# Latent attention on one Trainium2 core: value products issued for two steps at a time

## The chip, the cores and the metric

The kernel runs on 1 core of one Trainium2 chip. The metric is device time in microseconds (us). The engines are TensorE (PE in the rows, its weight loads PEld), VectorE (DVE), ScalarE (ACT), GpSimd (POOL) and SyncE (SP). The time before is 3274.03 us, the median of three runs (3273.06 to 3274.99).

## The reference, cut to what matters

The program is a two-layer block with three branches (convolution, mLSTM, latent attention) over 512 tokens and 256 context tokens, followed by a second block. Only the attention is touched: 8 heads, queries and keys of 64 plain and 32 rotated features, values of 64 features.

```python
def mla_attend(qn, qr, kn, kr, v):
    s = jnp.einsum('bqhd,bkhd->bhqk', qn, kn) + jnp.einsum('bqhr,bkr->bhqk', qr, kr)
    p = jax.nn.softmax(s.astype(jnp.float32) * MLA_SCALE, axis=-1).astype(v.dtype)
    return jnp.einsum('bhqk,bkhd->bqhd', p, v)
...
    o_x = mla_blockwise(qn_x, qr_x, jnp.concatenate([kn_c, kn_x], 1), jnp.concatenate([kr_cc, kr_x], 1),
                        jnp.concatenate([vv_c, vv_x], 1))
...
    o_c = mla_attend(qn_c, qr_c, kn_c, kr_cc, vv_c).reshape(bsz, uc.shape[1], MLA_HEADS * V_HEAD)
```

The last line (attention of the context tokens over themselves) is computed in the first layer only.

## The kernel before

`attention_stage(core, l)` is run for layer 0 (`both` is true: tokens and context are queries) and for layer 1 (tokens alone). The eight heads go in four pairs p = 0 to 3; j = 0 and 1 is the head in the pair. Keys go in six tiles of 128, and each key tile is one **step** i of its pair: i = 0 to 5. In layer 0 a seventh step, i = 6, holds the context queries (`items` is 7 there, 6 in layer 1). g counts the steps through all pairs: 28 in layer 0, 24 in layer 1.

What one step does, each part named by its function:

- `score(g, j)`: the scores of head j, transposed (128 keys x 512 queries) in one PSUM bank per head. Pair 0 uses plain fp32 (L1676); the other pairs split queries and keys in a high and a low part and add three fp32r products (L1679, L1680, L1681). It waits for the exponential of the same head one step before (`exp_ready`, at 2g - 1 + j), which frees the bank.
- `exponent(g, j)` on ACT (L1795): exponential of the bank into one of four `probs` tiles, tile (2g + j) % 4. From g = 2 on it first waits until the value products of step g - 2 are done (`attended`, at g - 1) and until the sums of step g - 2 are added.
- `add(g, j)` on POOL (L1914, L1917; L1910 for the context): the running sum of the exponentials, from which the softmax's denominator comes.
- `attend(g)`: the value products, probabilities times values. Both heads write one bank, head 0 in partitions 0 to 63 and head 1 in 64 to 127 (L1732; L1739 for the context step, i = 6). Each of the two products shows in the trace as two matmuls, so a step shows as four.
- `unit(p + 1, u)`: the rough scores of the next pair, from which the row maxima come (L1618, for the context L1622), one or two per step (`units_of`). Unit u waits for the maximum of unit u - 2. `maximum` on DVE (L1964) reads each one. The last of them lets `turn_rows` (L1631) put the maxima on the queries' rows; ACT and DVE copy the rows (L1815, L1969), and the next pair's first scores wait for these copies.
- `total(p, ctx)`: the sums of the exponentials over the partitions (L1718). In layer 1 it stands in step 1 of the next pair, and after the last step.
- In layer 0 steps 2 and 4 hold modulation products as well (`mod_rows_pair`, L787, and `turn_mods`, L796); a `turn_mods` of a pair before the last waits for the third or fifth maximum of its pair.

DVE also computes the low parts of the next pair (`query_low` L1973, `key_low` L1978), reciprocals of the sums (L2000) and copies of results and totals (L1985, L1994), in the fixed order in which they are written. ACT rounds the next pair's queries and keys (L1800, L1805) in steps 0 and 1; unit 0 waits for that.

The order on PE is written out by hand in one loop over g: `score(g, 0)`, first unit, `score(g, 1)`, `attend(g - 1)`, second unit, and what the step has besides. So the value products run one step behind the scores:

```python
            score(g, 1)
            if g:
                attend(g - 1)
            if second is not None:
                unit(p + 1, second)
```

Of the kernel before, what the change touches and what calls it, by code (L numbers as in the profile page):

```python
# [1439 lines left out]
def attention_stage(core, l):  # L1440

    nc, both = core.nc, l == 0
# [53 lines left out]
    def at_group(kind, n):  # L1497

        g = HEAD_GROUPS[l].index((kind, n))
        return g // 4, g % 4  # L1500
# [9 lines left out]
    steps_of = [(p, i) for p in range(PAIRS) for i in range(items)]  # L1510
# [5 lines left out]
    def unit_at(p, i, j):  # L1516

        return units_of.get(i, (None, None))[j] if p + 1 < PAIRS else None
# [9 lines left out]
    mod_steps = [g for g, (p, i) in enumerate(steps_of) if both and i in (2, 4)]  # L1528
    n_steps = len(mod_steps)
    assert 2 * n_steps == n_mods  # L1530
    halves = [(0, TC), (TC, TX)]
    lows_at = {1: [("query", 0)], 3: [("key", 0)], 4: [("query", 1)], 5: [("key", 1)]} if both else \
        {2: [("query", 0), ("key", 0)], 4: [("query", 1), ("key", 1)]}
# [14 lines left out]
    def _(pe):  # L1548
# [10 lines left out]
        def turn_mods(b):  # L1559
            pe.wait_ge(mod_copied.sem, mod_copied.at(b + 1))  # L1560
            return turn_mod_rows(core, pe, lambda pair: mod_rows, 1, mod_sums[:, 4 * b:4 * b + 4])
# [121 lines left out]
        def score(g, j):  # L1683
            p, i = steps_of[g]
            if g:
                pe.wait_ge(s["exp_ready"].sem, s["exp_ready"].at(2 * g - 1 + j))
            elif j == 0:

                pe.wait_ge(s["v_copied"].sem, s["v_copied"].at(1))
                pe.wait_ge(s["v_copied_by_act"].sem, s["v_copied_by_act"].at(1))  # L1690
            copied = s["odd_rows_copied" if j else "rows_copied"]
            if i == 0:
                pe.wait_ge(copied.sem, copied.at(row_sets * p + 1))
                if j == 0:
                    pe.wait_ge(s["kr_copied"].sem, s["kr_copied"].at(2 * p + 2))
                if in_parts[p]:
                    for low in (s["query_low"], s["key_low"]):
                        pe.wait_ge(low.sem, low.at(2 * p - 2 + j + 1))
            if i < NT:
                mm = scored_tile(scores[j], p, j, slice(i * P, (i + 1) * P), slice(0, TX))  # L1700
            else:
                pe.wait_ge(copied.sem, copied.at(row_sets * p + 2))
                for x in range(NT - NTX):
                    mm = scored_tile(scores[j][:, x * TC:(x + 1) * TC], p, j, slice(TX + x * P, TX + (x + 1) * P), slice(TX, T))
            mm.then_inc(s["scored"].sem, 1)

        def total(p, ctx):

            n = p * closings + ctx
            pe.wait_ge(s["added"].sem, s["added"].at(adds_until(p, NT if ctx else NT - 1, 1)))  # L1710
            last_ctx = ctx and p + 1 == PAIRS
            if both and not ctx:
                pe.wait_ge(mod_copied.sem, mod_copied.at(2 * p + 2))
            if n and not last_ctx:
                pe.wait_ge(s["totals_copied"].sem, s["totals_copied"].at(n))
            for j in range(2):
                source, to = (ctx_sums[j], last_totals if last_ctx else totals[:, 0:TC]) if ctx else (sums[j], totals)
                mm = pe.matmul(to[j * VH:(j + 1) * VH, :], core.ones[:, 0:VH], source, start=True, stop=True, skip_group_check=True)  # L1718
            mm.then_inc(s["totaled"].sem, 1)

        def attend(g):
            p, i = steps_of[g]
            n = p * closings
            pe.wait_ge(s["exp_ready"].sem, s["exp_ready"].at(2 * g + 2))
            if g == 0:
                pe.wait_ge(s["v_copied"].sem, s["v_copied"].at(3))
                pe.wait_ge(s["v_copied_by_act"].sem, s["v_copied_by_act"].at(3))
            if i < NT:
                if i == 0 and p:
                    pe.wait_ge(s["result_copied"].sem, s["result_copied"].at(n))  # L1730
                for j in range(2):
                    mm = pe.matmul(result[j * VH:(j + 1) * VH, :], values[:, i, 2 * p + j, :], probs[(2 * g + j) % 4],  # L1732
                                   start=(i == 0), stop=(i == NT - 1), skip_group_check=True)
            else:
                if p + 1 < PAIRS:
                    pe.wait_ge(s["result_copied"].sem, s["result_copied"].at(n + 1))
                for x in range(NT - NTX):
                    for j in range(2):
                        mm = pe.matmul(ctx_results[p][j * VH:(j + 1) * VH, :], values[:, NTX + x, 2 * p + j, :],  # L1739
                                       probs[(2 * g + j) % 4][:, x * TC:(x + 1) * TC], start=(x == 0), stop=(x == NT - NTX - 1),  # L1740
                                       skip_group_check=True)
            mm.then_inc(s["attended"].sem, 1)

        for g, (p, i) in enumerate(steps_of):
            first, second = unit_at(p, i, 0), unit_at(p, i, 1)
            score(g, 0)
            if p and i == 1 and not both:
                total(p - 1, 0)
            if i == items - 1 and p + 1 < PAIRS:
                turn_rows(p + 1, 0)  # L1750
            if first is not None:
                if g == 1:
                    pe.wait_ge(s["v_copied_by_act"].sem, s["v_copied_by_act"].at(3))
                unit(p + 1, first)
            score(g, 1)
            if g:
                attend(g - 1)
            if second is not None:
                unit(p + 1, second)
            if both and i == NT:  # L1760
                total(p, 0)
            elif both and i == 0 and p:
                total(p - 1, 1)
            if g in mod_steps:
                b = mod_steps.index(g)
                if b:
                    if p + 1 < PAIRS:
                        pe.wait_ge(s["max_ready"].sem, s["max_ready"].at((p + 1) * len(units) + (3 if i == 2 else 5)))
                    turn_mods(b - 1)
                else:  # L1770
                    pe.wait_ge(s["v_copied"].sem, s["v_copied"].at(3))
                if p:
                    pe.wait_ge(s["totals_copied"].sem, s["totals_copied"].at(closings * p))
                mod_rows_pair(core, pe, run, *at_group("mod", 2 * b), mod_in)
            if i == 0 and both:
                turn_rows(p, 1)
        attend(len(steps_of) - 1)
        total(PAIRS - 1, closings - 1)
        if both:
            turn_mods(n_steps - 1).then_inc(mod_turned.sem, 1)  # L1780
# [3114 lines left out]
```

## Time and profile before

| what | before |
|---|---|
| median of three runs | 3274.03 us (3273.06 to 3274.99) |
| the profiled execution's own time | 3270.61 us |
| its span | 3268.8 us |
| PE busy | 3169.7 us, 97% of the span |
| DVE / POOL / ACT busy | 2012.1 / 1199.2 / 1182.1 us |
| steps of the attention in layer 0 | 397 to 508 us of the span |
| steps of the attention in layer 1 | 1819 to 1907 us of the span |

The span is that of one execution under the profiler. A row of the timeline gives the start in us from the span's start, how long the merged instructions took together, the engine, the line of the kernel, what they write and read, their number, and in brackets how long the engine had been idle and what released it. Starts of matmuls are the better guide: the end of one is modelled, and it overlaps the next.

### The profile page before, as it was taken

How to read it: one execution, taken by the hardware profiler on the slowest of the kernel's cores; microseconds unless marked ns; L12 is line 12 of the kernel's file. 1: busy time of each engine (PE TensorE's matmuls, PEld its weight loads, DVE VectorE, ACT ScalarE, POOL GpSimd, SP SyncE). 2: the span in 40 equal slices, each digit the busy share in tenths (PEclk: the TensorE clock that was granted, in tenths of full speed). 3: DMA queues.
4: the chain of work that ended last, by engine and by line, in shares of the span. 5: the costliest groups of instructions: out<-in, count | busy, mean ns of one | idle time of the engine just before them, and what ended most of it. 6: DMA issues, size and time to landing. Idle time of an engine off the chain costs nothing. (4 is left out here: it accounts for less than half of the span.)

```text
span 3268.8 us, 46548 instructions
## 1 busy us (share of the span) xinstructions
PE 3169.7 (97%) x17058; PEld 2552.7 (78%) x17058; DVE 2012.1 (62%) x2954; ACT 1182.1 (36%) x1672; POOL 1199.2 (37%) x607
## 2 busy tenths in 40 slices
PE   8999999999999999999999989999999998999998
PEld 7888557888888888887776467778998766788886
DVE  6957565448877424257996653678533675777634
ACT  3232444522243223133543444234322364322223
POOL 3332155233333222232431453543444314344442
PEclk9999999999999999999999999999999999999999
DMA  6222120234412222222222003652333221333332
GB/s 227 58 58 52 48 78 20 55 103 152 147 57 66 60 63 65 62 62 72 76 78 55 7 1 110 195 172 85 97 91 97 78 77 52 91 96 90 94 98 79
DMA packets 467677, 271.75 MB, mean 83 GB/s; under 512 B 53937, under 2 KB 453297, under 8 KB 466354
## 3 DMA queue, kind: packets, MB, share of 16 engines
q1 hardware_dynamic: 467362, 269.36, 28.0%
q8 instruction: 119, 1.95, 0.3%
q14 instruction: 52, 0.43, 0.0%
q10 hardware_dynamic: 144, 0.02, 0.0%
HBM read 267.21 MB, written 2.10 MB: 82 GB/s over the span
## 5 line engine op out<-in xcount | busy, mean ns | idle before, releaser
L390 POOL TENSOR_TENSOR weights_low<-weight_ring,weights_high 128x1024 fp32r<-128x1024 f32 (+1 forms) x403 | 979.4, 2431 | 1719.7 <-ACT weights_high L381 1718.6
L381 ACT ACTIVATE weights_high<-weight_ring 128x1024 fp32r<-128x1024 f32 (+1 forms) x408 | 410.2, 1006 | 1071.2 <-PE ps L491 1006.8
L486 PE MATMUL ps<-features_high,weights_high 128*128 128x512 f32 (+1 forms) x1888 | 638.9, 353 | 8.3 <-DVE features_low L2759 4.6
L487 PE MATMUL ps<-features_low,weights_high 128*128 128x512 f32 (+1 forms) x1888 | 635.2, 353 | 0.0
L486 PEld LDWEIGHTS ps<-features_high,weights_high 128*128 128x128 f32 x1888 | 355.0, 188 | 68.1 <-DVE features_low L2759 5.7
L487 PEld LDWEIGHTS ps<-features_low,weights_high 128*128 128x128 f32 x1888 | 354.7, 188 | 55.0 <-issue 0.2
L491 PE MATMUL ps<-features_high,weights_low 128*128 128x512 f32 (+1 forms) x1888 | 384.3, 351 | 0.0
L486 PE MATMUL ps<-u_high,weights_high 128*128 128x512 f32 (+2 forms) x944 | 369.5, 395 | 8.8 <-DVE z L3814 2.6
L487 PE MATMUL ps<-u_low,weights_high 128*128 128x512 f32 (+2 forms) x944 | 363.0, 389 | 0.0
L491 PEld LDWEIGHTS ps<-features_high,weights_low 128*128 128x128 f32 x1888 | 305.3, 188 | 47.3
L1337 DVE SCALAR_TENSOR_TENSOR conv<-conv,vectors 128x512 f32<-128x512 f32 (+1 forms) x480 | 307.2, 707 | 5.5 <-DVE conv L1337 3.9
L486 PE MATMUL ps<-mlp_u_high,weights_high 128*128 128x512 f32 (+1 forms) x960 | 269.2, 310 | 0.9 <-DVE arena L3604 0.9
L487 PE MATMUL ps<-mlp_u_low,weights_high 128*128 128x512 f32 (+1 forms) x960 | 267.1, 310 | 0.0
L3546 DVE SCALAR_TENSOR_TENSOR x_features<-ps,modulation,x_features 128x512 f32<-128x512 f32 x118 | 74.9, 661 | 266.1 <-PE ps L491 254.6
L491 PE MATMUL ps<-u_high,weights_low 128*128 128x512 f32 (+2 forms) x944 | 227.8, 384 | 0.0
L486 PEld LDWEIGHTS ps<-u_high,weights_high 128*128 128x128 f32 (+1 forms) x944 | 180.1, 191 | 56.1 <-issue 10.9
L487 PEld LDWEIGHTS ps<-u_low,weights_high 128*128 128x128 f32 (+1 forms) x944 | 180.1, 191 | 39.5 <-issue 1.4
L491 PEld LDWEIGHTS ps<-u_high,weights_low 128*128 128x128 f32 (+1 forms) x944 | 171.0, 188 | 38.3 <-issue 0.5
L486 PEld LDWEIGHTS ps<-mlp_u_high,weights_high 128*128 128x128 f32 x960 | 180.9, 188 | 13.7 <-ACT weights_high L381 1.0
L487 PEld LDWEIGHTS ps<-mlp_u_low,weights_high 128*128 128x128 f32 x960 | 180.7, 188 | 10.8
L3482 ACT ACTIVATE arena<-arena,seam 128x512 f32<-128x512 f32 x96 | 59.1, 647 | 287.4 <-DVE arena L3628 287.4
L491 PE MATMUL ps<-mlp_u_high,weights_low 128*128 128x512 f32 (+1 forms) x960 | 150.9, 309 | 0.0
(638 smaller groups left out, 4960.9 us busy)
## 6 DMA issues: line engine op xcount, KB each, us to landing
weight_ring<-in_w SPq DMA_DIRECT2D x256, 256.0 KB, 3.0
weight_ring<-in_w_in SPq DMA_DIRECT2D x246, 256.0 KB, 3.3
conv<-in_w_mod_columns SPq DMA_DIRECT2D x64, 512.0 KB, 4.7
weight_ring<-in_w_up SPq DMA_DIRECT2D x88, 256.0 KB, 3.1
weight_ring<-in_w_out SPq DMA_DIRECT2D x48, 256.0 KB, 3.1
weight_ring<-in_w_mod SPq DMA_DIRECT2D x32, 256.0 KB, 3.5
weight_ring<-in_w_down SPq DMA_DIRECT2D x32, 256.0 KB, 3.0
first_modulation<-in_first_modulation SPq DMA_DIRECT2D x4, 1024.0 KB, 9.5
```

The lines of the kernel that those rows point to most:

```text
L381: act.activation(core.ring_high[:, split_slot(run, q), 0:n], core.ring[:, slot, 0:n], ACT.Copy).then_inc(core.high_ready.sem, 1)
L390: pool.tensor_tensor(core.ring_low[:, split_slot(run, q), 0:n], core.ring[:, (run.first + q) % SLOTS, 0:n], high.bitcast(F32), ALU.subtrac ...
L486: pe.matmul(to, w_high[:, k, 0:m], high(k, a, b), start=(first and k == ks[0]), stop=False, skip_group_check=True)
L487: pe.matmul(to, w_high[:, k, 0:m], low(k, a, b), start=False, stop=False, skip_group_check=True)
L491: mm = pe.matmul(out[:, at:at + b - a], w_low[:, k, 0:m], high(k, a, b), start=False, stop=(last and k == ks[-1]), skip_group_check=True)
L1337: nc.vector.scalar_tensor_tensor(conv[:, f, a:b], pads[:, f, bass.ds(t + at, b - a)], w_dw[:, bass.ds(t, 1), f], conv[:, f, a:b], ALU.mult ...
L3482: ins = act.activation(tmp[:, a:b], pre_of[own(i, q)][:, a:b], ACT.Relu, bias=cols_of[own(i, q)][:, ns + j:ns + j + 1])
L3546: ins = nc.vector.scalar_tensor_tensor(x, gemm(core, q % 2)[:, a:b], mod[:, gates + q, j:j + 1], x, ALU.mult, ALU.add)
```

## The change

The value products are no longer issued in every step. A table of the step's number i says which steps' products stand behind `score(g, 1)`: at i = 2 and i = 4 (and i = 6 in layer 0) those of the two steps before, one behind the other; at i = 0 in layer 1 those of the last two steps of the pair before, in layer 0 the context step's alone. At i = 1, 3 and 5 there are none. In layer 1 the last two steps' products stand together behind the loop, as they did before. Nothing else is moved, and waits and buffers are as they were.

```diff
+    values_behind = lambda g: [] if g == 0 else {0: [g - 1] if both else [g - 2, g - 1], 2: [g - 2, g - 1], 4: [g - 2, g - 1],
+                                                 6: [g - 2, g - 1]}.get(steps_of[g][1], [])
...
             score(g, 1)
-            if g:
-                attend(g - 1)
+            for of in values_behind(g):
+                attend(of)
             if second is not None:
...
-        attend(len(steps_of) - 1)
+        for of in [len(steps_of) - 1] if both else range(len(steps_of) - 2, len(steps_of)):
+            attend(of)
         total(PAIRS - 1, closings - 1)
```

In the changed kernel the lines behind the table are two higher (L1734 is the old L1732, L1681 to L1683 are L1679 to L1681, L1620 is L1618). The names: L1679 to L1681 are one head's scores, L1618 a unit, L1732 the value products, L1718 the totals, L1631 `turn_rows`.

PE in layer 1, third pair (p = 2), from the second head's scores of step 3 to those of step 5, before:

```order
L1679 MATMUL ps<-query_part_13156,features_high 128x512
L1680 MATMUL ps<-features_low,features_high 128x512
L1681 MATMUL ps<-query_part_13156,features_high 128x512
L1732 MATMUL ps<-ranks 64x512 x2
L1618 MATMUL ps<-weights_high,weights_low 128x512
L1618 MATMUL ps<-weights_high,weights_low 128x256
L1679 MATMUL ps<-features_low,features_high 128x512
L1680 MATMUL ps<-features_low,features_high 128x512
L1681 MATMUL ps<-features_low,features_high 128x512
L1618 MATMUL ps<-weights_high,weights_low 128x512
L1618 MATMUL ps<-weights_high,weights_low 128x256
```

The same place in the changed kernel, one step further, to the second head's scores of step 4, the value products and the second unit behind them:

```order
L1681 MATMUL ps<-query_part_13156,features_high 128x512
L1682 MATMUL ps<-features_low,features_high 128x512
L1683 MATMUL ps<-query_part_13156,features_high 128x512
L1734 MATMUL ps<-ranks 64x512 x4
L1620 MATMUL ps<-weights_high,weights_low 128x512
L1620 MATMUL ps<-weights_high,weights_low 128x256
```

In step 3 the products are gone; in step 4 four stand between the second scores and the last unit, where two stood.

PE in layer 1 at the passage from the third pair to the last, from `turn_rows` of step 5 to the value products of the next step 0, before:

```order
L1631 MATMUL ps<-constants,conv 33x128 x4
L1679 MATMUL ps<-query_part_13156,features_high 128x512
L1680 MATMUL ps<-features_low,features_high 128x512
L1681 MATMUL ps<-query_part_13156,features_high 128x512
L1732 MATMUL ps<-ranks 64x512 x2
L1679 MATMUL ps<-weights_low,weights_high 128x512
L1680 MATMUL ps<-features_low,weights_high 128x512
L1681 MATMUL ps<-weights_low,features_high 128x512
L1679 MATMUL ps<-weights_low,weights_high 128x512
L1680 MATMUL ps<-features_low,weights_high 128x512
L1681 MATMUL ps<-weights_low,features_high 128x512
L1732 MATMUL ps<-ranks 64x512 x2
```

and in the changed kernel:

```order
L1633 MATMUL ps<-constants,conv 33x128 x4
L1681 MATMUL ps<-query_part_13156,features_high 128x512
L1682 MATMUL ps<-features_low,features_high 128x512
L1683 MATMUL ps<-query_part_13156,features_high 128x512
L1681 MATMUL ps<-weights_low,weights_high 128x512
L1682 MATMUL ps<-features_low,weights_high 128x512
L1683 MATMUL ps<-weights_low,features_high 128x512
L1681 MATMUL ps<-weights_low,weights_high 128x512
L1682 MATMUL ps<-features_low,weights_high 128x512
L1683 MATMUL ps<-weights_low,features_high 128x512
L1734 MATMUL ps<-ranks 64x512 x4
```

The products of step 4 moved from behind the scores of step 5 to behind those of the next pair's step 0, beside the products of step 5.

## Rows read from the trace of the kernel before

**Rows 1.** The page, busy time and instructions of each engine.
```profile
PE 3169.7 (97%) x17058; PEld 2552.7 (78%) x17058; DVE 2012.1 (62%) x2954; ACT 1182.1 (36%) x1672; POOL 1199.2 (37%) x607
```

**Rows 2.** Windows, one pair of each kind: third of layer 0, second and last of layer 1.
```profile
core 0: us, PE busy (x) PEld busy (x) DVE busy (x) ACT busy (x) POOL busy (x), PEclk, DMA share, GB/s
455.00:484.00 29.00, 27.75 (x190) 16.52 (x188) 21.28 (x24) 13.43 (x22) 18.31 (x14) 1.00 0.26 74
1842.00:1864.00 22.00, 20.94 (x89) 10.51 (x88) 17.17 (x17) 10.24 (x17) 14.84 (x12) 1.00 0.00 1
1886.00:1907.00 21.00, 19.07 (x74) 8.04 (x72) 5.67 (x7) 7.16 (x12) 15.05 (x12) 1.00 0.00 1
```

**Rows 3.** Timeline of PE, layer 1: scores, value products alone, then together, totals.
```profile
1889.16 0.40 PE L1680 MATMUL ps<-features_low,weights_high 96*128 96x512 f32 x1
...
1893.90 0.40 PE L1681 MATMUL ps<-weights_low,features_high 96*128 96x512 f32 x1
1894.23 1.08 PE L1732 MATMUL ps<-ranks 128*64 128x512 f32 x4
1895.24 0.50 PE L1679 MATMUL ps<-weights_low,weights_high 97*128 97x512 f32 x1
1895.58 0.40 PE L1680 MATMUL ps<-features_low,weights_high 96*128 96x512 f32 x1
1895.81 0.39 PE L1681 MATMUL ps<-weights_low,features_high 96*128 96x512 f32 x1
...
1902.05 1.94 PE L1732 MATMUL ps<-ranks 128*64 128x512 f32 x8
1905.76 1.08 PE L1718 MATMUL ps<-ranks,ones 128*64 128x512 f32 x4 [1.78 <-POOL ranks L1917]
```

**Rows 4.** Timeline of DVE, layer 1, third pair.
```profile
1869.09 0.96 DVE L1964 TENSOR_REDUCE conv<-ps 128x1 f32<-128x768 f32 x1 [1.75 <-PE ps L1618]
1869.97 0.68 DVE L1994 COPY conv<-ps 128x512 f32<-128x512 f32 x1
1871.34 0.96 DVE L1964 TENSOR_REDUCE conv<-ps 128x1 f32<-128x768 f32 x1 [0.69 <-PE ps L1618]
1872.21 1.74 DVE L2000 RECIPROCAL conv<-conv 128x256 f32<-128x256 f32 x1
1873.87 1.75 DVE L1964 TENSOR_REDUCE conv<-ps 128x1 f32<-128x768 f32 x2
...
1881.49 1.75 DVE L1964 TENSOR_REDUCE conv<-ps 128x1 f32<-128x768 f32 x2
```

**Rows 5.** Timeline of PE, layer 1, third pair: products, second unit; later `turn_rows`.
```profile
1872.97 1.08 PE L1732 MATMUL ps<-ranks 128*64 128x512 f32 x4
1873.98 0.62 PE L1618 MATMUL ps<-weights_high,weights_low 96*128 96x512 f32 x2
...
1883.29 1.06 PE L1631 MATMUL ps<-constants,conv 128*33 128x128 f32 x8 [0.64 <-DVE conv L1964]
```

**Rows 6.** Timelines of ACT and of POOL, layer 1, last pair.
```profile
1893.64 1.30 ACT L1795 ACTIVATE ranks<-ps 128x512 f32<-128x512 f32 x2 [1.31 <-PE ps L1681]
1896.24 1.30 ACT L1795 ACTIVATE ranks<-ps 128x512 f32<-128x512 f32 x2 [1.31 <-PE ps L1681]
...
1894.31 7.73 POOL L1917 TENSOR_TENSOR ranks<-ranks 128x512 f32<-128x512 f32 x6 [0.63 <-ACT ranks L1795]
1902.00 1.27 POOL L1923 TENSOR_TENSOR features<-features,conv 128x512 f32<-128x512 f32 x1
1903.23 2.48 POOL L1917 TENSOR_TENSOR ranks<-ranks 128x512 f32<-128x512 f32 x2
```

**Rows 7.** Timelines, layer 0: PE in the first pair; DVE, then PE in the third.
```profile
421.62 1.06 PE L1631 MATMUL ps<-constants,conv 128*33 128x128 f32 x8 [0.19 <-DVE conv L1964]
...
459.36 1.75 DVE L2000 RECIPROCAL conv<-conv 128x256 f32<-128x256 f32 x1
461.14 0.96 DVE L1964 TENSOR_REDUCE conv<-ps 128x1 f32<-128x768 f32 x1
...
478.10 0.28 PE L1681 MATMUL ps<-features_low,features_high 96*128 96x256 f32 x1
479.62 1.06 PE L1631 MATMUL ps<-constants,conv 128*33 128x128 f32 x8 [1.25 <-DVE conv L1964]
...
481.77 1.08 PE L1732 MATMUL ps<-ranks 128*64 128x512 f32 x4
```

**Rows 8.** A wait of PE, and windows around it and behind the first attention.
```profile
1714.04 1.18 PE L1104 MATMUL ps<-constants,arena 36*128 36x36 f32 x16 [1.92 <-ACT gates L1216]
...
1716.20:1722.90 6.70, 6.70 (x28) 5.90 (x28) 6.08 (x12) 0.00 (x0) 1.17 (x1) 0.50 0.01 2
477.00:481.00 4.00, 2.75 (x21) 2.27 (x20) 3.74 (x5) 0.87 (x2) 4.00 (x4) 1.00 0.52 152
```

## The prediction

> **What bounds the kernel now.** I read the busy times first [rows 1]: PE is busy for 97% of the span, so time is saved where PE gets shorter and lost where PE waits. The change lies in two stretches, 397 to 508 us and 1819 to 1907 us, about 6% of the span. The windows [rows 2] show PE busy for 27.75 of 29, 20.94 of 22 and 19.07 of 21 us there. That is an average, so I went on to the timelines, to see which wait ends last at each place. Two other engines are close. In layer 1's third pair DVE starts its second maximum at 1871.34 and from then on runs one operation behind the other until the last maximum, which ends at 1883.24 [rows 4]; 0.05 us later `turn_rows` starts, at 1883.29, after PE waited [rows 5]. So from the second unit to `turn_rows` DVE sets the time. In layer 1's last pair POOL adds, divides and adds without a gap from 1894.31 to 1905.71, and the total on PE starts at 1905.76 after waiting 1.78 us for it [rows 3, 6]. That tail is POOL's.
>
> **What one merge saves.** [rows 3] have both cases. Score products follow each other at 0.23 us (1895.58 to 1895.81). A value block alone begins 0.33 us after the last score product (1893.90 to 1894.23), the next product starts 1.01 us after the block (1895.24), and the one after that 0.34 us later (1895.58) in place of 0.23. So a block alone puts 0.33 + 1.01 - 0.23 + 0.11 = 1.22 us between scores. Behind the last step two blocks already touch: eight matmuls take 1.94 us, four take 1.08, so the second costs 0.86. A merge saves 1.22 - 0.86 = 0.36, say 0.35 us. In layer 0, 24 blocks become 12; in layer 1, 23 become 12, since the last two touch already. 12 + 11 merges by 0.35 are 8.0 us: the most that the change can give, 0.25% of the run.
>
 Taken as the whole story, the rule makes this the first rival below.
>
> **Layer 0, pair 0** (397 to 426 us). PE sets the pace (even `turn_rows` waits only 0.19 us for DVE [rows 7]), so its three merges pay 1.05 us. But `turn_rows` in step 6 waits for DVE, and what stood ahead of it and could be hidden is moved behind it: going through the steps with 1.22 and 0.86 I get the first unit pairs earlier, the last maximum 1.5 us earlier, and the next pair's first scores 0.7 us earlier. **-0.7 us.**
>
> **Layer 0, pairs 1 and 2.** Here `turn_rows` waits 1.25 us for the last maximum (478.10 plus 0.28 against 479.62) [rows 7]. In step 5 the value products of step 4 stand in that wait's shadow and cost nothing. After the change they stand behind `turn_rows`, beside those of step 5, and cost 0.86. Ahead of it DVE is limited by its own order: the merge of step 2 buys nothing, because unit 2, which now comes sooner, waits for the first maximum, and that one stands behind a reciprocal of 1.75 us [rows 7]; the merge of step 4 brings DVE forward by some 0.25 us. 0.86 - 0.25 = 0.6 us each, two pairs: **+1.2 us.**
>
> **Layer 0, pair 3** has no units and no `turn_rows`. Three merges would give 1.05 us. But a new wait appears: `exponent(g, 0)` needs the value products of step g - 2, which in an even step now stand behind `score(g, 1)`. The next scores of that head need this exponential. From the start of two blocks, the first is done after about 1.07 us and the exponential after another 0.65; the scores come 1.87 us after the start. That fits with 0.1 us to spare. In the odd steps scores come two after two with no products between. A head's scores start at 1895.24 and their exponential at 1896.24 [rows 3, 6]: 1.0 us, and 0.65 for the exponential, make a round trip of 1.65, while PE has 0.8 + 0.7 = 1.5 us of scores to fill it. That is 0.15 us of waiting, two or three times in the pair. I leave -0.45 us. **Layer 0 together: -0.7 + 1.2 - 0.45 = 0.05 us.**
>
> **Layer 1, pairs 0 and 1.** In pair 0 the merges are eaten by unit 6, which waits for the maximum of unit 4 once units come sooner; the next pair begins 0.26 us early. Through pair 1 the same DVE chain holds, with unit 1 over 1 us earlier (no products ahead of it) and the last unit as late as before behind two blocks. At the end of it the lead is about 0.15 us. The double block (steps 4 and 5) then stands in step 0 of pair 2, ahead of unit 0.
>
> **Layer 1, pair 2.** Unit 0 comes 0.86 - 0.15 = 0.7 us later, and its maximum starts at 1869.8 in place of 1869.09. The totals' copy stands behind it [rows 4], so the second maximum starts at 1871.3, as before, although its unit is there earlier. In step 2 the second unit stands behind two blocks: it starts at 1874.3 in place of 1873.98 [rows 5], and the fourth maximum 0.3 us later, since DVE had started that one almost at once. Unit 6 waits for the fifth maximum and inherits the 0.3; the double block of step 4 follows, and unit 7 ends only about 1883.1, where DVE would have begun its maximum at about 1882.3 [rows 4]. So `turn_rows` starts about 0.85 us late, at 1884.15, and behind it the double block costs another 0.86: the first scores of step 1 of the last pair are 1.7 us late.
>
> **Layer 1, pair 3.** Step 1 has no products now, so PE makes good 1.0 us: the scores of step 2 are only 0.65 us late (1893.3). But their exponential no longer follows them. It waits for the first of the two value blocks behind the second head's scores: those scores at 1894.1, the block at 1894.9, done 1.07 us later, so the exponential starts at 1896.0 in place of 1893.64, and POOL's first add at 1896.65 in place of 1894.31 [rows 6], 2.35 us late. From there POOL has the same six adds, one division and two adds, 11.4 us without a gap. The total starts 2.35 us late, and the stage ends with it. **Layer 1: +2.35 us.** No later merge can win it back, since POOL, not PE, ends this stage.
>
> **The sum.** 0.05 + 2.35 = 2.4 us. The profiled execution took 3270.61 us itself, which would become 3273.0; it lies 3.4 us under the median of the runs, 3274.03, and against that the forecast is **3276.4 us**. A measurement of this kernel can tell about 0.2%, 6.5 us, from no change, so the likeliest outcome is none that can be told. No instruction, transfer or queue entry is added; SP's order and its waits for free weight slots are the same, and the modulation weights' slots come free within 0.5 us of before. Bounds of the unknown part: the round trip of an exponential could cost nothing (then pairs 3 of both layers keep their merges: layer 0 0.6 us better, layer 1 still tied to POOL), or 0.3 us more at each of the 24 double blocks, 7 us worse. The DVE stretches could give 1 us back or take 1 us more.
>
> **Rivals.**
>
> *A. PE keeps every merge* (chance 0.12). The drains go away and neither DVE nor POOL is in the way: 3274.03 - 8.0 = 3266.0 us. For it: PE is busy 97%, and no row shows DVE at work for a whole pair (17.17 of 22 us [rows 2]). Against it: `turn_rows` waits for DVE in the later pairs of both layers, and the total waits for POOL [rows 3, 5, 7].
>
> *B. The longer waits bring TensorE's clock down* (chance 0.13). In layer 0, pairs 1 and 2, PE reaches step 6 earlier while `turn_rows` stays with DVE: its wait of 1.25 us grows to about 2.4. Today the granted clock stays at 1.00 over that wait; but a single wait of 1.92 us at 1714.04 is followed by 6.7 us at 0.50, 1.2 GHz in place of 2.4 [rows 8]. PE work in such a stretch takes twice as long, so each costs up to 3.4 us. Twice: 3276.4 + 6.8 = 3283.2 us, 0.28% slower than before. It decides if the wait reaches about 1.9 us and the clock's check falls on it. Against it: PE is dense on both sides of the wait.
>
> The Trainium skill (TensorE: Matmul & The Clock Gate, What's actually happening) says that TensorE's clock is set by how busy it was recently. [rows 8] agree for the wait at 1714; whether this wait is enough no row shows.
>
> *C. The POOL tail does not grow* (chance 0.2): the start of the last pair is less late than I think, or POOL finds gaps to close. Then the gains and losses cancel: 3274 us.
>
> That the change does not do what it says is excluded: the order on PE shows the four products together in the even steps.
>
> **How the numbers follow.** My forecast has 0.55 (3272 to 3279.5 us by itself), A 0.12, B 0.13, C 0.2. Faster by over 0.2% is A, 0.12; slower by over 0.2% is B, 0.13; the rest, 0.75, lies within 0.2%. The range reaches from 3268.5, which leaves out the full gain of A, to 3283.5, which takes in B.
>
> **What would show it.** Right: a value block of eight matmuls in 1.94 us everywhere; `turn_rows` in layer 1's third pair 0.8 us later after the pair's start than now; the first add of POOL's closing run 2.3 us later than now and the run still 11.4 us without a gap; PE's wait before `turn_rows` in layer 0's third pair about 2.4 us; first scores of the last pair in layer 0 some 0.5 us later. Wrong: a stage in layer 1 that ends earlier than 1906.8, a granted clock under 1.00 inside either stretch, or exponentials that hold up the scores in every even step.

## The result, and the profile after

The changed kernel took 3296.13 us (median of 4 runs, 3293.77 to 3296.55), the kernel before beside it 3273.66 us (4 runs, 3273.06 to 3274.99): **a ratio of 1.0066, 95% interval 1.0051 to 1.0081, 22.5 us slower.** That lies beyond the range of the prediction. The profiled execution took 3293.77 us with a span of 3291.9.

The two traces run level (within 0.15 us) up to the first attention. Behind layer 0's attention PE is 6.2 us late, at the first product behind layer 1's 21.9 us; at the end of the span it is 23.1. So nearly the whole loss lies in the two stretches that the change touches. I measure a stage from its first `turn_rows` to the first product of what follows: layer 0 goes from 120.6 to 127.0 us, layer 1 from 95.6 to 111.3 us.

The page of the changed kernel answers to [rows 1]: as many instructions as before, but PE is busy for 9.3 us longer, since part of the same work now runs at a lower clock.

```profile
PE 3179.0 (97%) x17058; PEld 2560.7 (78%) x17058; DVE 2019.4 (61%) x2954; ACT 1179.3 (36%) x1672; POOL 1201.2 (36%) x607
```

Windows over the two attention stages before, columns as in [rows 2]:

```profile
399.00:513.90 114.90, 106.12 (x706) 59.07 (x706) 69.86 (x80) 48.74 (x82) 66.92 (x55) 0.99 0.26 73
1815.70:1911.30 95.60, 85.07 (x329) 39.05 (x329) 56.82 (x56) 40.14 (x67) 58.22 (x44) 0.98 0.02 6
```

and the same of the changed kernel, then three windows inside them:

```profile
398.80:520.10 121.30, 109.45 (x706) 63.24 (x706) 71.31 (x80) 47.44 (x82) 64.62 (x55) 0.93 0.24 69
1821.90:1933.20 111.30, 90.62 (x329) 42.31 (x329) 63.03 (x56) 38.71 (x66) 60.38 (x44) 0.91 0.02 5
...
455.00:484.00 29.00, 26.21 (x182) 16.40 (x179) 19.93 (x22) 13.11 (x22) 17.35 (x14) 0.97 0.26 74
449.00:455.80 6.80, 6.31 (x22) 3.83 (x24) 2.70 (x4) 0.38 (x1) 0.51 (x1) 0.50 0.01 2
1892.80:1899.60 6.80, 6.00 (x14) 2.33 (x15) 4.08 (x4) 1.09 (x2) 2.03 (x2) 0.50 0.00 0
```

Two things stand out. The mean granted clock (the column PEclk) falls from 0.99 to 0.93 and from 0.98 to 0.91: there are six new stretches at 0.50, which is 1.2 GHz in place of 2.4, two in layer 0 (449.0 and 483.1, 6.8 us each) and four in layer 1 (1841.6, 1869.0 and 1906.5, 3.4 us each, and 1892.8, 6.8 us). And DVE is busy for 6.2 us more in layer 1, with no more work to do.

PE's timeline of the changed kernel shows a longer wait just ahead of each of those stretches, or around its start. First `turn_rows` of layer 0's third pair, which answers to [rows 7], and the products behind it; then unit 6 of layer 1's third pair, with score products and a value block behind it; then the last total, which answers to [rows 3]:

```profile
479.44 0.28 PE L1683 MATMUL ps<-features_low,features_high 96*128 96x256 f32 x1
482.19 1.06 PE L1633 MATMUL ps<-constants,conv 128*33 128x128 f32 x8 [2.47 <-DVE conv L1967]
483.18 0.80 PE L1624 MATMUL ps<-weights_high,weights_low 96*128 96x256 f32 x2
...
1890.70 0.39 PE L1683 MATMUL ps<-features_low,features_high 96*128 96x512 f32 x1
1893.60 1.01 PE L1620 MATMUL ps<-weights_high,weights_low 96*128 96x512 f32 x2 [2.51 <-DVE conv L1967]
1894.40 0.63 PE L1681 MATMUL ps<-query_part,features_high 97*128 97x512 f32 x1
1894.83 0.63 PE L1682 MATMUL ps<-features_low,features_high 96*128 96x512 f32 x1
1895.82 3.68 PE L1734 MATMUL ps<-ranks 128*64 128x512 f32 x8
...
1927.68 1.08 PE L1720 MATMUL ps<-ranks,ones 128*64 128x512 f32 x4 [2.67 <-POOL ranks L1920]
```

A block of eight value products takes 3.68 us behind that wait, and 1.94 us where the clock is at 1.00. The other three stretches of layer 1 stand at waits of 1.98 us (unit 6 of the first pair, 1841.39), 2.48 us (unit 6 of the second, 1867.89) and 1.71 us. The last of these is at a place that the prediction didn't look at: behind `turn_rows` the second head's first scores wait for DVE's copy of the row of maxima (L1972, the old L1969):

```profile
1905.62 0.47 PE L1681 MATMUL ps<-weights_low,weights_high 97*128 97x512 f32 x1 [1.71 <-DVE weights_low L1972]
```

DVE's timeline, layer 1, third pair, shows what unit 6 waited for:

```profile
1888.32 0.96 DVE L1967 TENSOR_REDUCE conv<-ps 128x1 f32<-128x768 f32 x1 [0.32 <-PE ps L1620]
1889.19 1.54 DVE L1976 TENSOR_TENSOR features_low<-features,weights_low 96x512 fp32r<-96x512 f32 x1
1890.66 2.02 DVE L1981 TENSOR_TENSOR features_high<-features,weights_high 96x768 fp32r<-96x768 f32 x1
1892.60 1.81 DVE L1967 TENSOR_REDUCE conv<-ps 128x1 f32<-128x768 f32 x2
```

The two tensor-tensor operations form the low parts of queries and keys (`query_low`, `key_low`). In the first pair of the kernel before, DVE does the same shapes in 0.68 and 0.95 us:

```profile
1838.41 0.68 DVE L1973 TENSOR_TENSOR features_low<-features,weights_low 96x512 fp32r<-96x512 f32 x1
1839.01 0.95 DVE L1978 TENSOR_TENSOR features_high<-features,weights_high 96x768 fp32r<-96x768 f32 x1
```

POOL's timeline of the changed kernel has at that time four adds in one run, over both operations; and in the last pair the closing run, which answers to [rows 6]:

```profile
1887.65 6.15 POOL L1920 TENSOR_TENSOR ranks<-ranks 128x512 f32<-128x512 f32 x4 [1.86 <-ACT ranks L1798]
...
1916.33 7.63 POOL L1920 TENSOR_TENSOR ranks<-ranks 128x512 f32<-128x512 f32 x6 [1.43 <-ACT ranks L1798]
1923.92 1.26 POOL L1926 TENSOR_TENSOR features<-features,conv 128x512 f32<-128x512 f32 x1
1925.15 2.48 POOL L1920 TENSOR_TENSOR ranks<-ranks 128x512 f32<-128x512 f32 x2
```

In the kernel before, POOL's adds of the second pair (and of the third, 22.3 us later) come as two and, 0.8 us behind them, three; query's low part (1853.25 to 1853.93) lies in the gap between them but for its last 0.2 us, and key's runs into the three:

```profile
1850.42 2.52 POOL L1917 TENSOR_TENSOR ranks<-ranks 128x512 f32<-128x512 f32 x2 [0.98 <-ACT ranks L1795]
1853.74 4.60 POOL L1917 TENSOR_TENSOR ranks<-ranks 128x512 f32<-128x512 f32 x3 [0.80 <-ACT ranks L1795]
```

ACT's timeline of the changed kernel has the source of the run of four. Two exponentials, which wait for the merged value products, follow each other at once, and two more come behind them; before they stood 1.05 us apart or more:

```profile
1886.97 1.09 ACT L1798 ACTIVATE ranks<-ps 128x512 f32<-128x512 f32 x2 [1.31 <-issue]
1889.03 0.60 ACT L1798 ACTIVATE ranks<-ps 128x512 f32<-128x512 f32 x1 [0.97 <-PE ps L1683]
1890.08 0.60 ACT L1798 ACTIVATE ranks<-ps 128x512 f32<-128x512 f32 x1 [0.46 <-PE ps L1683]
```

### The profile page after: what moved, and what is told of

Its sections match the earlier page's. It is cut to its first block and busy times, and to the rows that moved or that the text cites. A ratio compares the mean times of both kernels' runs of the same rounds, so it can differ in the third digit from the quotient of the medians.

```text
span 3291.9 us, 46548 instructions
## 1 busy us (share of the span) xinstructions
PE 3179.0 (97%) x17058; PEld 2560.7 (78%) x17058; DVE 2019.4 (61%) x2954; ACT 1179.3 (36%) x1672; POOL 1201.2 (36%) x607
```

## The experiments

Three causes are weighed: that the granted clock falls behind longer waits; that DVE and POOL hinder each other, since the adds are bunched; and that only the order on PE costs, as in the prediction.

### One layer at a time

```diff
+    merged = values_behind
+    values_behind = merged if both else (lambda g: [g - 1] if g else [])    (layer0_only)
+    values_behind = (lambda g: [g - 1] if g else []) if both else merged    (layer1_only)
-        for of in [len(steps_of) - 1] if both else range(len(steps_of) - 2, len(steps_of)):
+        for of in [len(steps_of) - 1]:                                      (layer0_only)
```

> The merged order in layer 0 alone, layer 1 as before. The changed kernel's trace is 6.2 us behind the old one from the end of layer 0's attention on, with two new stretches of 6.8 us at a granted clock of 0.50 in pairs 1 and 2. Theory (the two attentions are independent): 3273.7 + 6 = about 3280 us, with those two stretches again. Rival (the whole 22 us comes from how later clock stretches fall after a shift): 3290 us or more, or none of it.

> The merged order in layer 1 alone, layer 0 as before. Theory: 3273.7 + 16 = about 3290 us; waits of PE of about 2.5 us before the seventh unit of pairs 1 and 2, and stretches of low clock behind them. Rival (phase only): since layer 0 does not shift the later part by 6 us, the low stretches fall elsewhere and the cost is under 8 us.

Measured: layer 0 alone 3279.79 us (3277.35 to 3282.10, 10 runs) against 3275.67 (17 runs), ratio 1.0012 [1.0003, 1.0022]; layer 1 alone 3289.22 us (3284.24 to 3293.49, 6 runs), 1.0037 [1.0024, 1.0049]. So 4.1 and 13.6 us: each layer's part makes the kernel slower, the second by more, and the untouched layer keeps its length (95.66 and 120.63 us). The two do not add up to 22.5 us. The traced execution of layer 1 alone was the slowest of its six; its stage took 114.6 us, with five low stretches where the changed kernel has four in 111.3. In the profile of layer 0 alone the clock fell in one pair only, 124.1 us for the stage in place of 127.0. That gives a comparison of two like pairs in one execution, the second and the third, same order, with and without the low clock:

```profile
429.70:462.60 32.90, 30.10 (x190) 18.17 (x188) 20.60 (x24) 13.09 (x23) 17.37 (x14) 0.90 0.22 64
462.60:492.40 29.80, 27.02 (x190) 16.86 (x188) 20.65 (x24) 12.42 (x22) 17.38 (x14) 1.00 0.25 72
```

One fall costs 3.1 us. It came in one of two like places. The runs of these kernels also scatter by 5 and 9 us, which would fit with falls that come in one execution and not in another; only one execution of each has a trace, so that is not shown.

### The changed order, with the waits filled

Head 0's score products are issued again just ahead of the longer waits; they write the same values once more, so PE is at work where it had been idle. The first attempt also repeated second heads' scores in layer 0, behind the wait; the second one doesn't.

```diff
+            again = (1 if j else 4 if p in (1, 2) and i == NT else 1) if both else
+                {(0, 4): 3, (1, 4): 4, (2, 4): 4, (1, 0): 2, (2, 0): 2, (3, 0): 2}.get((p, i), 1) if j == 0 else 1
-                mm = scored_tile(scores[j], p, j, slice(i * P, (i + 1) * P), slice(0, TX))
+                for _ in range(again):
+                    mm = scored_tile(scores[j], p, j, slice(i * P, (i + 1) * P), slice(0, TX))
```

> The changed order in both layers, but where PE would wait it repeats the products of the first head's scores (which its exponential does not follow at once in those steps), 2 to 4 times over, so that PE has work in the waits. Theory clock (the longer waits bring the clock down and the work behind them runs at 1.2 GHz): the new low stretches, 30.6 us in all, vanish, and with them 10 to 15 us: 3281 to 3286 us. What is left over 3274 is the order's own cost on DVE and POOL. Rival order (DVE and POOL chains set the whole loss and the clock falls only where nobody waits for PE): 3294 us or more, as the repeats only add work.

> The changed order with PE kept busy in its waits, this time with the first head's scores alone repeated (in the first such kernel layer 0's second heads were repeated too, behind the wait, at 2.1 us in each of two pairs). Theory clock plus order: no stretch of low clock inside either attention; layer 0's stage 0.5 us longer than before (121.1 us against 120.63 from the first row turn to the next stage), layer 1's 8 us longer (104 against 95.6). About 3282 us. Rival (the order costs nothing once the clock stays up): 3274 to 3276 us.

Measured: the first 3286.41 us (3282.89 to 3288.34, 6 runs) against 3275.67, 1.0028 [1.0016, 1.0041]; the second 3284.01 us (3280.61 to 3284.68, 6 runs) against 3274.31 (12 runs), 1.0032 [1.0019, 1.0044]. Neither has a low stretch in an attention before its end. Windows of the second one over both stages, and over layer 1's second and third pair:

```profile
399.00:514.20 115.20, 107.72 (x741) 64.62 (x740) 71.38 (x79) 47.26 (x81) 64.64 (x54) 0.99 0.26 73
1816.30:1920.30 104.00, 90.88 (x361) 46.24 (x360) 63.36 (x57) 38.76 (x67) 60.49 (x44) 0.98 0.02 6
1840.70:1865.50 24.80, 23.44 (x100) 13.31 (x101) 19.21 (x18) 10.02 (x18) 14.60 (x11) 1.00 0.00 1
1865.50:1890.20 24.70, 23.17 (x101) 13.32 (x101) 19.16 (x18) 9.78 (x18) 16.09 (x12) 1.00 0.00 1
```

With 67 more products recorded on PE the kernel loses 9.7 us to the one before in place of 22.5. So the clock's part is shown, in both layers. By stage, filling takes 6.0 us from layer 0 (126.96 to 120.97) and 7.3 from layer 1 (111.34 to 104.01): 13.3 us, beside 12.8 in the medians. What is left is 0.34 us in layer 0 and 8.4 in layer 1, and the clock can't explain those: it stands at 1.00 up to the last value products. Nor do the repeated products add to PE's path in layer 1: PE still waits for DVE behind them, 0.27 to 0.43 us before unit 6 and 0.6 to 0.75 us before the second heads' first scores.

### POOL's adds made short, in either order

From the third step of a pair on, the adds cover 32 of 512 columns, and the add of the second step only copies one operand, scaled by 1. What is left out are the sums of the exponentials over the steps.

```diff
-                ins = nc.gpsimd.tensor_tensor(sums[j], probs[(2 * g - 2 + j) % 4], here, ALU.add)
+                ins = nc.gpsimd.tensor_scalar(sums[j], here, 1.0, None, ALU.add)
...
-                ins = nc.gpsimd.tensor_tensor(sums[j], sums[j], here, ALU.add)
+                ins = nc.gpsimd.tensor_tensor(sums[j][:, 0:32], sums[j][:, 0:32], here[:, 0:32], ALU.add)
```

> The old order; GpSimd's running sums are left out but for 32 of 512 columns (from a pair's third step on), so that GpSimd is nearly idle while VectorE makes the low parts; the output is not the reference's. Theory contention (VectorE's low parts take 1.5 and 2.0 us in place of 0.7 and 0.95 when GpSimd adds at the same time): key parts in layer 1 at 0.95 us, the stage in layer 1 shorter than 95.6 us by 3 to 6 us, the last 1.8 us of them from GpSimd's tail. Rival (they are slow for another reason): 2.0 us as before.

> The same shortened sums in the changed order. Theory contention: query and key parts at 0.7 and 0.95 us; layer 1's stage, apart from low clock, within 3 us of that of the old order with shortened sums, where it is 8.4 us over with full sums. Rival (the order of the products alone holds PE up, through VectorE's fixed order and the exponentials): still 6 us or more over.

Measured (one run each, so I read the stages and not the times, 3271.13 and 3270.86 us): layer 1 takes 91.63 us in the old order and 91.22 in the new one. With short adds the new order is 0.4 us *shorter*; with full adds, and the clock held up, it is 8.4 us longer. Layer 0 takes 118.93 and 122.37 us, the latter with one fall of the clock in it, which cost some 3 us.

Windows over layer 1's stage, old order, then new order:

```profile
1817.50:1909.20 91.70, 84.40 (x330) 39.55 (x329) 52.12 (x57) 40.18 (x67) 25.53 (x44) 0.99 0.02 6
```

```profile
1820.00:1911.20 91.20, 82.60 (x330) 40.47 (x329) 52.64 (x57) 38.74 (x67) 25.85 (x44) 1.00 0.02 6
```

DVE's low parts in the third pair, new order with short adds, and below it the same place in the second pair of the filled kernel with full ones:

```profile
1863.95 0.97 DVE L1976 TENSOR_TENSOR features_low<-features,query_part 96x512 fp32r<-96x512 f32 x1
1864.85 1.00 DVE L1981 TENSOR_TENSOR features_high<-features,features_high 96x768 fp32r<-96x768 f32 x1
```

```profile
1856.25 1.53 DVE L1978 TENSOR_TENSOR features_low<-features,features_low 96x512 fp32r<-96x512 f32 x1
1857.70 2.04 DVE L1983 TENSOR_TENSOR features_high<-features,features_high 96x768 fp32r<-96x768 f32 x1
```

So layer 1's 8.4 us hang on POOL's full adds. The repeated products are not the reason: the changed kernel without them has the same long low parts. The twelve low parts of the stage take 14.8 us before, 20.9 in the changed kernel, 21.3 in the filled one; with short adds they take 10.0 in the old order and 10.6 in the new. A third way, that the exponentials wait for the sums, shows in none of these five traces: where an exponential waits in this stage, its wait is never put down to POOL. Two ways are left, which this pair of kernels doesn't part. The low parts are 6.5 us longer. And the closing run starts later, which the last pair's distance from `turn_rows` to the total shows: 22.5 us before, 24.6 filled, +2.1.

Longer low parts also delay what stands behind them on DVE. The copy of the row of maxima is behind two of them, and in the filled kernel the second head's first scores wait for it in each of three pairs:

```profile
1869.61 0.47 PE L1681 MATMUL ps<-query_part,features_high 97*128 97x512 f32 x1 [0.75 <-DVE query_part L1974]
```

In the kernel before and with short adds no such wait is over 0.25 us.

The Trainium skill (SBUF — State Buffer, Summary: rules for kernel authors) says that a VectorE instruction with two inputs in SBUF contends with a GpSimd instruction that reads SBUF, and that the later of the two blocks fully until the first is done. This case agrees: the same shape takes 0.68 or 1.5 us, 0.95 or 2.0 us. In the changed kernel the query's low part of 1889.19 starts while an add runs that ends at 1890.18, and ends itself 0.55 us behind it; and POOL loses time as well, with 6.15 us for the four adds beside both low parts where six without low parts beside them take 7.63.

### The low parts moved to another step

On the filled kernel, layer 1's first two low parts stand in step 3 in place of step 2, away from the bunched adds.

```diff
-        {2: [("query", 0), ("key", 0)], 4: [("query", 1), ("key", 1)]}
+        {3: [("query", 0), ("key", 0)], 4: [("query", 1), ("key", 1)]}
```

> The changed order with the waits filled (first heads repeated), and in layer 1 VectorE makes the first head's low parts one step later, in step 3, behind that step's maxima and reciprocal, when GpSimd has finished the four adds that now come in one run. Theory contention: these low parts take 0.7 and 0.95 us in place of 1.5 and 2.0, and layer 1's stage is 3 to 5 us shorter than 104.0 us, 99 to 101 us. Rival (it is the position in VectorE's order that costs, or the repeated scores): within 1 us of 104.

```profile
1867.45 0.62 DVE L1978 TENSOR_TENSOR features_low<-features,features_low 96x512 fp32r<-96x512 f32 x1
1867.99 0.94 DVE L1983 TENSOR_TENSOR features_high<-features,features_high 96x768 fp32r<-96x768 f32 x1
```

In the second pair (DVE's timeline, above) and in the third the moved ones take 0.62 and 0.94 us; the others still 1.5 and 2.04. From the first `turn_rows` to the last total the stage takes 96.6 us in place of 98.5. Contention holds in its direction, but 1.9 us is less than the 3 to 5 that I had expected, although the twelve low parts together fell by 5.1 us, from 21.3 to 16.2. So most of that time was not on the path. The second ones still meet the adds, and the wait for the row copy behind them stays (0.60 to 0.74 us). The single run, 3288.44 us, is not to be read: the clock was low in further places, outside the attentions too.

### The old order, with a longer wait

Does a longer wait alone bring the clock down, without any merge? Layer 0's last maximum is made late in two pairs by two more reductions into unused columns; then the same with the wait filled by head 0's scores, four times.

```diff
+            for spare in range(2 if both and u == 7 and p in (2, 3) else 0):
+                nc.vector.tensor_reduce(small_max[:, 38 + spare:39 + spare], source, AX.X, ALU.max, negate=True)
```

> The old order with two reductions more on VectorE ahead of the last row maximum, in layer 0's pairs 1 and 2, which lengthens PE's wait before the row turn from 1.25 to about 3.0 us (2 x 0.87). Theory clock (a longer wait of PE alone brings the clock down): in these pairs low stretches of 6.8 us behind the wait, costing about 3 us each beside the 1.75: 3275.7 + 3.5 + 6 = 3285 us. Rival (the wait alone does not do it): 3279 us, no low stretch.

> The old order with the two reductions more in layer 0's pairs 1 and 2, and the first head's context scores repeated three times more there, 2.1 us of products inside the 3.0 us wait. Theory clock: no low stretch in the attention; the stage in layer 0 is 120.63 + 3.5 = 124.1 us, against 128.08 without the repeats; 3278 us. Rival (the low stretches were chance): a stretch in one of the two pairs, 126 us or more.

Measured: 3283.37 us (3281.36 to 3288.01, 7 runs) against 3274.31, 1.0031 [1.0019, 1.0042]; filled 3280.16 us (3275.89 to 3287.72, 10 runs) against 3274.21 (27 runs), 1.0019 [1.0009, 1.0028]. PE's timeline of the first of these kernels, at layer 0's second pair, and the window that begins with it:

```profile
453.66 1.89 PE L1631 MATMUL ps<-constants,conv 128*33 128x128 f32 x8 [2.99 <-DVE conv L1966]
...
453.70:457.10 3.40, 3.40 (x15) 2.80 (x16) 2.15 (x3) 0.58 (x1) 0.00 (x0) 0.50 0.00 0
```

and the same place, filled:

```profile
453.52 1.06 PE L1631 MATMUL ps<-constants,conv 128*33 128x128 f32 x8 [0.85 <-DVE conv L1968]
```

With the wait, both pairs have a low stretch and the stage takes 128.08 us; filled, none and 124.08 us. So in the old order too, the wait brings the clock down, and 2.0 us a pair come back when PE repeats work there. The filled kernel's time is 2 us above the 3278 that I had expected; the stage's length is the expected one.

### Only the places where nobody waits

Merged in layer 0's first and last pair alone:

```diff
-    values_behind = (the table of the change)
+    values_behind = lambda g: merged(g) if both and steps_of[g][0] in (0, 3) else [g - 1] if g else []
```

> The merged order only in layer 0's pairs 0 and 3, where PE sets the pace; everything else as before. Theory: each merge saves 0.35 us there: layer 0's stage 119.3 us in place of 120.63 (1.05 in pair 0, 0.3 in pair 3), layer 1's 95.6, no low stretch inside either. Rival (the merge saves nothing by itself): 120.6 us.

Measured: layer 0's stage 119.26 us, 1.37 less than before; layer 1 as before, 95.64. The time of its single run, 3272.35 us, can't tell 1.4 us.

### The stage ends kept busy

Both kernels before and after have low stretches behind each attention, at 511.2 and 1907.3 us of the trace before, where PE stands still: for 5.29 us behind the last products of layer 0, and in layer 1 for 1.78 us ahead of the last total and 4.47 us behind it. Here PE repeats products of an identity there (five at each end, two ahead of layer 1's last total), once on the old order and once on the one above.

```diff
+        def busy(n):
+            for _ in range(n):
+                pe.matmul(scores[0], core.ident, core.base[:, 0:512], start=True, stop=True, skip_group_check=True)
+        if not both:
+            busy(2)
         total(PAIRS - 1, closings - 1)
...
+        busy(5)
```

> The old kernel, but PE repeats a product of constants into a free bank while it would wait at the end of each attention: five fp32 products (about 4.3 us) after the last one, and two before layer 1's last total. Theory clock: the two low stretches behind the attentions (6.8 us each, at 511 and 1907 us) go or get shorter; 2 to 4 us less, 3271 us. Rival (the idle time that brings the clock down is elsewhere, or what runs there does not wait for PE): no change.

> Both of these together: if both theories hold, 3 to 5 us less than before, 3270 us. Rival: no change.

> The merges in layer 0's pairs 0 and 3 with PE kept busy at the ends of both attentions, measured once more: its first interval reached from 0.17% faster to 0.01% slower. Theory: 1.4 us from the merges and up to 3 us from the clock, ratio 0.9990. Rival: no difference, ratio 1.0000.

Measured: alone 3273.08 us (3270.63 to 3276.63, 11 runs) against 3274.21 (27 runs), 0.9998 [0.9989, 1.0007]; with the merges 3271.58 us (3269.05 to 3275.17, 11 runs), 0.9992 [0.9983, 1.0001]; the latter again, against another set, 3270.49 us (3268.33 to 3274.93, 11 runs) against 3274.67 (15 runs), 0.9986 [0.9977, 0.9995]. Windows of that run over layer 0's stage and behind each attention, where the trace before has 0.50:

```profile
394.60:510.70 116.10, 111.72 (x727) 62.75 (x727) 71.58 (x78) 50.70 (x84) 66.54 (x54) 1.00 0.28 78
510.70:518.00 7.30, 6.41 (x44) 4.89 (x43) 6.11 (x12) 3.86 (x5) 3.04 (x4) 1.00 0.01 2
1904.00:1914.00 10.00, 9.70 (x52) 6.06 (x52) 7.28 (x10) 3.76 (x5) 3.06 (x5) 1.00 0.00 1
```

The low stretches there are gone. Alone, their removal changes no time that the medians can tell: the 2 to 4 us that I had expected are not to be seen in them. The traces do show a gain at the place itself. From the last total of layer 0 to one and the same VectorE operation behind it, before, then with the ends kept busy:

```profile
507.66 0.60 PE L1718 MATMUL ps<-rope,ones 128*64 128x256 f32 x4
538.45 0.60 DVE L2211 SCALAR_TENSOR_TENSOR ranks<-ranks 128x4 f32<-128x4 f32 x1
```

```profile
509.08 0.60 PE L1718 MATMUL ps<-rope,ones 128*64 128x256 f32 x4
537.84 0.60 DVE L2217 SCALAR_TENSOR_TENSOR ranks<-ranks 128x4 f32<-128x4 f32 x1
```

That is 28.8 us in place of 30.8, 2.0 us less. It is 30.0 to 31.3 in all twelve traces without these products and 28.8 in all three with them. Behind layer 1 a like distance from the last total is 24.9 in place of 25.9, with that total 0.1 us later. So the low stretches cost some 2.9 us there. The mean clock of the whole trace is still 0.990 (0.991 before), since short falls come at other places; whether these took the gain back is not shown.

Merges and fillers together are some 2.6 to 4.2 us faster than the kernel before, beside 1.4 for the merges and 2.9 for the ends by the traces, with an interval that leaves 1 out in one of the two measurements. It is the fastest order tried, by little.

## Why the prediction was wrong

The forecast, no change that can be told (3276.4 us), was wrong, and the time fell outside the range. By its own steps:

- **What one merge saves: right.** Eight products take 1.94 us, and in layer 0's first and last pair, where I saw little waiting, the merges save 1.37 us: 1.05 and 0.31 us (I had 0.7 and 0.45, 1.15 together).
- **Layer 0 without the clock: nearly right, in part by luck.** The filled kernel's stage is 0.34 us longer than before (I had 0.05). By pairs it is -1.06, +0.86, +0.83 and -0.30 us, where I had -0.7, +0.6, +0.6 and -0.45: the misses cancel in part. The moved block costs 0.86 us behind `turn_rows` as worked out: from it to the context's `turn_rows` PE takes 8.4 to 8.6 us in place of 7.6 to 7.7. The 0.25 us that the merge ahead of it was to give back didn't come. PE's wait there is 2.47 us, where I had written about 2.4.
- **Rival B, the clock: the mechanism was right, its chance and its places were wrong.** I had worked out the wait of 2.4 us, had a row in which 1.92 us was followed by a clock of 0.50 [rows 8], and still gave it 0.13, with "PE is dense on both sides of the wait" as the reason. (The row was no clean case: between that wait and the fall PE had only products of 36x36 and 4x6.) And I put it at layer 0's pairs 1 and 2 alone. In layer 1 I had written that unit 6 "waits for the fifth maximum" and took this for a delay only, never asking how long PE then stands still: it is 1.98, 2.48 and 2.51 us in the three pairs. The wait for the row copy, up to 1.71 us, I had not seen at all. Both layers together, the clock costs some 13 us, of which I had 6.8, in a case that I hardly counted.
- **The layer 1 term, +2.35 us: mis-sized, and this is where the forecast failed even without the clock.** It measures +8.4. The delay of POOL's closing run is right in kind and near in size: it lasts 11.3 us without a gap (1916.33 to 1927.63; I had 11.4), and from `turn_rows` to the total the last pair is 2.1 us longer, where I had 1.5. What failed is the step "through pair 1 the same DVE chain holds": each of the three pairs ahead is 1.6 to 2.4 us longer from one `turn_rows` to the next (24.4, 24.7 and 24.7 us in place of 22.9, 22.5 and 22.3). I had taken the durations of DVE's operations as fixed and moved only their starts. The trace before already had the sign: `key_low` takes 0.95 us in the first pair and 2.03 in the others, beside an add on POOL. In the second and third pair the low parts grow by 1.35 us, and 0.86 for the moved block would make 2.2, near the 2.3 and 2.4 measured. But that is an account that fits, not one that was shown part by part, and two runs speak against reading it as a plain sum: with short adds the same two pairs grow by only 0.1 us, although the block is moved there too, and with the first low parts moved away the twelve fell by 5.1 us and the stage by 1.9. In the first pair the low parts grow by 3.8 us and the pair only by 1.6. What is shown is the 8.4 as a whole, and that it goes with POOL's long adds.
- **The exponential's new wait: right, and its consequence was missed.** Two exponentials now wait for one merged block and come together. I followed this only in the last pair, for the time at which POOL starts. In the others it is what puts four adds side by side, 6.15 us of POOL over both of DVE's low parts, where before the query's slipped in between two adds and three.

What is left open: why a wait of about the same length is followed by a lower clock at one place and not at a like one; which of the waits in layer 1 costs how much, since they were only filled together; and how the 8.4 us divide among low parts, row copy and closing run.

## What to carry to other kernels

When an order is moved, list the engine's waits that grow and compare each with the waits in the same trace behind which the clock fell: where one comes to that length, the fall belongs in the forecast and not in a rival. Here that length was shorter than it seemed, with falls behind waits of 1.4 us and more. Then look at which other engines' work becomes bunched by the same order, and check each duration taken from the trace against its longest instance: two durations of one shape were here the sign of a neighbour, and the neighbour moved too. The gain of this change was to be had piece by piece, at the places where nobody waits.

## What the runs showed of the hardware that was not expected

- Inside the attentions of all these traces the granted clock stayed at 1.00 behind each wait of PE of 1.24 to 1.32 us (13 of them). From 1.40 to 2.99 us it fell at 15 of 17; the exceptions are one of 1.60 us and one of 2.47, each with a like wait in the same trace where it did fall. A fall costs some 3.1 us in a stretch that PE bounds.
- Idle PE time can be dearer than useless work: 67 repeated products, in the waits, gave back some 13 us.
- At the stage ends the low stretches of 6.8 us cost less, some 2.0 and 0.9 us by the traces; the medians alone can't tell it (0.9998 [0.9989, 1.0007]).
- A VectorE tensor-tensor operation of 96x512 takes 0.68 us alone and 1.5 beside GpSimd's adds of 128x512, one of 96x768 0.95 and 2.0. Beside the four adds both engines lose: 6.15 us for them, where six without DVE's low parts take 7.63.
